# Differential attention: both score products of a step issued before both masks

## What is computed

```python
def _diff_attention(q, k, v, lam_params, subln_gain, layer_idx):
    q = q.reshape(bsz, seq, DIFF_HEADS, 2, DIFF_HEAD_DIM)   # 4 heads, 2 parts, 64
    k = k.reshape(bsz, seq, DIFF_HEADS, 2, DIFF_HEAD_DIM)
    ...
        mask = key_chunk[None, :] <= query_chunk[:, None]
        s1 = jnp.einsum('bhqd,bhkd->bhqk', q1_b, k1).astype(jnp.float32) * scale
        s2 = jnp.einsum('bhqd,bhkd->bhqk', q2_b, k2).astype(jnp.float32) * scale
        p1 = jax.nn.softmax(jnp.where(mask, s1, -jnp.inf), axis=-1)
        p2 = jax.nn.softmax(jnp.where(mask, s2, -jnp.inf), axis=-1)
        p = p1 - lam * p2
        return jnp.einsum('bhqk,bhkv->bhqv', p.astype(v.dtype), v)
```

## Time and profile before

| | us |
|---|---|
| median of three runs | 2064.28 |
| the profiled execution | 2043.03 |
| its span | 2041.2 |
| TensorE matmul busy | 1872.1 (92%) |
| VectorE busy | 1099.8 (54%) |
| ScalarE busy | 444.7 (22%) |
| GpSimd busy | 1059.1 (52%) |

### The profile page before, as it was taken

How to read it: one execution, slowest core, us unless ns; L and a number is a source line. 1 busy time by engine, 2 the same in 40 slices (tenths; PEclk the granted TensorE clock), 3 DMA queues, 4 the chain that set the end, 5 groups by cost and what they waited for, 6 DMA issues and landing times.

```text
span 2041.2 us, 22212 instructions
## 1 busy us (share of the span) xinstructions
PE 1872.1 (92%) x8206; PEld 1486.8 (73%) x8206; DVE 1099.8 (54%) x1235; ACT 444.7 (22%) x869; POOL 1059.1 (52%) x588
## 2 busy tenths in 40 slices
PE   7988897899999979997999999999856699999997
PEld 5865575678888867756888888887644588888885
DVE  7997528573442675165626344840566555344266
ACT  3213524420110131152201011101432222011011
POOL 7542253366666655504666666665500056666662
PEclk9989998899999989988999999999967699999999
DMA  5321121133333322301333333332200023333331
GB/s 202 92 72 42 42 73 52 42 93 93 103 93 94 101 83 77 94 1 52 94 102 93 95 101 93 94 101 86 83 0 0 0 82 94 93 101 95 93 103 42
DMA packets 45036, 160.55 MB, mean 79 GB/s; under 512 B 5136, under 2 KB 5648, under 8 KB 44832
## 3 DMA queue, kind: packets, MB, share of 16 engines
q1 hardware_dynamic: 43776, 157.31, 25.6%
q10 hardware_dynamic: 1184, 2.16, 0.3%
HBM read 157.35 MB, written 2.10 MB: 78 GB/s over the span
## 4 chain that ended last, share of the span: by engine, by line
PE 81%; DVE 13%; ACT 3%; issue 2%; DMA 0%; DVEq 0%; SPq 0%; ACTq 0%
PE bank L325 19%; PE bank L326 19%; PE bank L327 19%; PE bank L360 2%; PE bank L361 2%; PE bank L362 2%; DVE bank L1278 2%; DVE AL L1181 2%; PE bank L380 1%; PE bank L381 1%; PE bank L382 1%; PE bank L723 1%; PE bank L434 1%; PE bank L557 1%; PE bank L800 1%
## 5 line engine op out<-in xcount | busy, mean ns | idle before, releaser
L255 POOL TENSOR_SCALAR WH<-RAW 128x1024 fp32r<-128x1024 f32 x292 | 316.6, 1084 | 925.4 <-PE bank L327 410.0
L260 POOL TENSOR_TENSOR WL<-RAW,WH 128x1024 fp32r<-128x1024 f32 x292 | 742.6, 2543 | 24.4
L325 PE MATMUL bank<-AH,WH 128*128 128x512 f32 x944 | 369.6, 391 | 0.0
L326 PE MATMUL bank<-AL,WH 128*128 128x512 f32 x944 | 367.7, 390 | 0.0
L327 PE MATMUL bank<-AH,WL 128*128 128x512 f32 x944 | 367.7, 390 | 0.0
L325 PE MATMUL bank<-HH,WH 128*128 128x512 f32 x848 | 331.8, 391 | 0.0
L326 PE MATMUL bank<-HL,WH 128*128 128x512 f32 x848 | 330.4, 390 | 0.0
L327 PE MATMUL bank<-HH,WL 128*128 128x512 f32 x848 | 330.3, 389 | 0.0
L1482 DVE TENSOR_TENSOR HL<-TMP,HH 128x512 fp32r<-128x512 f32 x96 | 238.6, 2486 | 4.0 <-ACT HH L1052 0.8
L1047 ACT ACTIVATE TMP<-bank 128x512 f32<-128x512 f32 x96 | 57.2, 596 | 777.9 <-PE bank L327 739.2
L1488 DVE TENSOR_TENSOR Y<-Y,bank 128x512 f32<-128x512 f32 x72 | 49.5, 688 | 309.3 <-PE bank L327 309.3
(11 more groups left out here) (284 smaller groups left out, 2279.7 us busy)
## 6 DMA issues: line engine op xcount, KB each, us to landing
RAW<-wstream SPq DMA_DIRECT2D x292, 512.0 KB, 3.5
X<-xT SPq DMA_DIRECT2D x4, 512.0 KB, 7.4
out<-Y SPq DMA_DIRECT2D x8, 256.0 KB, 2.2
TMP<-memT ACTq DMA_DIRECT2D x1, 1024.0 KB, 9.1
BF<-masks ACTq DMA_DIRECT2D x1, 352.0 KB, 3.4
MIX<-pool_w ACTq DMA_DIRECT2D x1, 256.0 KB, 3.6
VC<-vecs ACTq DMA_DIRECT2D x1, 159.5 KB, 4.5
GM<-gla_masks ACTq DMA_DIRECT2D x1, 128.0 KB, 4.1
```

Source lines behind the costliest of these rows:

```text
L255: nc.gpsimd.tensor_scalar(WH[:, s, :, :].rearrange("p k n -> p (k n)"), RAW[:, s, :], 1.0, 1.0, ALU.mult, ALU.mult).then_inc(sem("w_high"), 1)
L260: nc.gpsimd.tensor_tensor(WL[:, s, :, :].rearrange("p k n -> p (k n)"), RAW[:, s, :], f32(WH[:, s, :, :].rearrange("p k n -> p (k n)")), A ...
L325: mm(bank, WH[:, slot, k, :], h(k), start=(k == 0), stop=False)
L326: mm(bank, WH[:, slot, k, :], l(k), start=False, stop=False)
```

## The change

TensorE's `attention` now issues all score products of a step first and collects their last instructions; if a `masked` function is given, it then issues the mask of each part, and the semaphore increments are put on these. The differential attention's score function is split in two for that, so that its order in a step is product 0, product 1, mask 0, mask 1 in place of product 0, mask 0, product 1, mask 1. The memory attention gives no `masked` and has one part a step, so its order is the same.

```diff
-            def attention(p, scores, values, o_place):
+            def attention(p, scores, values, o_place, masked=None):
...
+                        banks = [B[a["sbanks"][(i % rot) * subs + s]] for s in range(subs)]
+                        last = [scores(a["steps"][i], s, banks[s]) for s in range(subs)]
+                        if masked:
+                            last = [masked(a["steps"][i], banks[s]) for s in range(subs)]
                         for s in range(subs):
-                            bank = B[a["sbanks"][(i % rot) * subs + s]]
-                            scores(a["steps"][i], s, bank).then_inc(sem(f"{p}_scores"), 1)
+                            last[s].then_inc(sem(f"{p}_scores"), 1)
...
             def dif_scores(st, s, bank):
                 h, qt, kl = st
                 r = slice(s * 64, s * 64 + 64)
-                mm(bank[:, 0:kl], Q[r, h, qt * P:(qt + 1) * P], K[r, h, 0:kl], start=True, stop=False)
+                return mm(bank[:, 0:kl], Q[r, h, qt * P:(qt + 1) * P], K[r, h, 0:kl], start=True, stop=False)
+
+            def dif_mask(st, bank):
+                kl = st[2]
                 return mm(bank[:, kl - P:kl], BF[:, 0, :], BF[:, 2, :], start=False, stop=True)
             attention("dif", dif_scores, lambda h, kb: V[:, kb, h * P:(h + 1) * P],
-                      lambda h, qt, bank: bank[:, qt * P:(qt + 1) * P])
+                      lambda h, qt, bank: bank[:, qt * P:(qt + 1) * P], dif_mask)
```

## The result

The changed kernel took 2033.08 us (median of four, 2031.67 to 2041.14), the kernel before beside it 2063.92: a ratio of 0.9879, with a 95% interval of 0.9832 to 0.9926. It is faster by some 25 us (by the ratio) to 31 us (between the medians), where 4.6 were forecast and 2055.0 was the lowest time of the range. The two profiled executions lie only 9.6 us apart in span (2031.6 against 2041.2), so there are two questions: where these 9.6 come from, and where the other 20.

What follows compares the result with a forecast made beforehand. TensorE was taken to bound the differential attention; -2.6 us in the first stretch and -2.0 in two head loops gave -4.6, span 2036.6, and with 21.25 us carried over 2059.7 us, range 2055.0 to 2066.5.

Steps and rivals of the forecast that it cites:

- Step 2: Differential attention's two score products: second product's first record starts with the first's second; first mask after 1.6 us (512 keys).
- 3r: A step's two score products take three record times, not four; a step sheds 0.31 to 0.63 us.
- 2r: Outermost bound for a step's two score products: both run wholly together, in two record times.
- rival E: Both score products of a step wholly together: -9.6 us at most, 2054.7 us or later; chance 0.05.
- the 0.10 us: Score records on TensorE: a cost before every record that follows one on other or equal array rows.
- A: Score products: only the load is hidden, no overlap; sum -0.75 us, 2063.5 us; chance 0.18.
- B: The diff does nothing for the score products, still four record times; sum +0.5 us, 2064.8 us; chance 0.20.
- Step 3: VectorE's two maxima run back to back behind the masks, 0.61 us apart: +0.55 us a head, loop 10.1 us.
- Step 1: TensorE's masks: the second starts 0.07 us after the first, saving 0.10 us a step.
- Rival D: Products overlap and the attention's half-clock dip is shortened or gone: -5.6 to -9.6 us, 2054.7 to 2058.7; chance 0.13.
- Rival C: Products overlap, but TensorE idles over 1 us a head and later heads lose clock: +7.2 us, 2071.5; chance 0.07.
- The tail: After the differential attention's last scores, from 907.86 to the copy at 911.84: keeps its 3.98 us.

Runs made afterwards that it cites:

- version on the same rows: Changed kernel with both products of a step reading rows 0 to 63, so another output; median 2044.32 us, ratio 0.9933.
- late whole-row version: Kernel before with each product over all 128 rows (another output) and VectorE's first maximum also waiting for the second mask; median 2035.45 us.

## Why the prediction was wrong, point by point

1. **The base, the dearest mistake.** The sum was made against the profiled execution, and the 21.25 us by which the median lay above it were carried over as something at the ends that the edit does not touch. They were half clock inside the stage that the edit rewrites: 17.7 of them stand in the two profiles of the kernel before. The prediction had the price of a head at half clock, and all of its timed runs (2063.56 to 2065.37) lay 20 us above the profile, but it put the two together nowhere. Against its own profile the forecast was -4.6, measured -9.6 in span and -12.7 in the stage. Against the profile of a 2063.52 us execution the stage gives -30.4. At like clock the kernels are some 6 us apart, so the size of the forecast was near only for the smaller part of the gain.
2. **Step 2, how far the products overlap.** Taken at 3r, with 2r as the outermost bound and 0.05 of the chance (rival E). Measured 2r. The reasoning was that a product's second record stands in front of the other's first; in the trace the first records go together. By row, the savings per head are 0.74 (256 keys) and 0.94 us (384), from first record to where the transposes could start, and 1.21 us (512) to the mask that VectorE waits for; 2.89 in all, where 1.62 were taken (0.41 + 0.52 + 0.63 + 0.06). Of these 0.52 went back, most of it into new waits: 0.17 before the 512-key transposes at 890.31, which now wait for VectorE's combination, and 0.19 before their value products at 892.84, which now wait for ScalarE's copy. The head came out at 9.37 us, not 10.14. The Trainium skill, "TensorE: Matmul & The Clock Gate", section "Part 3: Packing small matmuls — row/col tiling", says that matmuls of other row groups start together, and the trace agrees (two records at 893.93). Its other half, that starts and ends keep program order, led the prediction to 3r, and that is not what was measured: the two products took 2r, so either the records are not issued product by product or the order does not hold for them; the trace can't tell which. The estimate from its table, 2.6r, was too careful for two products; by the terms of rival E it would have been worth 2.0 us, not 1.5.
3. **Step 2, the 0.10 us.** It was put on every record. It is 0.10 on entering a run and as much on leaving it, so two records of a product were a run of two, and a fit over two sizes couldn't tell "once a record" from "twice a run". For A and B this undersized the saving, as the version on the same rows showed (1.92 us for what B had at 2.1). The exception of the prediction, "the same cost with no change of mode", falls with it: inside a run no record paid the 0.10 us.
4. **Step 3, the late signal, was right.** One more maximum, 0.61 us, was forecast (+0.55 a head, with a first mask 0.06 earlier); by itself it cost 0.59 on whole rows (9.55 to 10.14) and 0.60 on the kernel before (11.15 to 11.75), and in the changed kernel the two maxima took 1.20 us where one took 0.61. It is 0.60 of the 1.05 us by which TensorE's idle time before the 384-key transposes rose (0.43 to 1.48 us). The rest is that the 128-key products, which fill part of that wait, now take 0.5 us less.
5. **Step 1** was right: the second mask follows the first by 0.06 us (894.99 to 895.05), and the transposes follow 0.12 us behind the first (895.11).
6. **The clock.** Rival D, the dip gone, had 0.13 and came true together with E (0.05); D was priced from the short dip, 5 us, E with the dip left as it was. Rival C, that idle TensorE lets the clock fall again for whole heads, is not borne out: the changed kernel idles 1.48 us a head and held 1.00 in one profile, the late whole-row version idles 1.56 and held it. A small part of it may be real: the three stretches of 3.4 us in the other profile of the changed kernel each began right behind a wait of 1.1 us or more, and made the stage 3.4 us longer. The prediction said that the clock went down in a stretch without idle time, but drew nothing from it for the length of the dip. What the runs show is that the long fall came in all four profiles with the old order on row halves in the first head, and in none of the eight others. In later heads the old order kept the full clock (41.6 us of it in the kernel with a changed first head), so half rows one after the other are not enough by themselves. Whether the rows bring the fall about, or the 0.10 us on entering and on leaving each run of them, is not separated: the same-rows version, half rows in fewer runs, held the clock in its first head and then lost it for 3.4 to 6.8 us at a time, 20.4 in all. Why one program can go either way after the fall stays open.
7. **The tail** kept its 3.98 us (897.84 to 901.82), as said.

## What to carry to other kernels

Before summing against a profiled execution, ask whether its time is that of the median; if not, the difference belongs to the sum, and the stretch where the clock is low with the engine busy is where it lay here. Here two products that use different row halves of the array and different banks cost one when they were next to each other (1.06 us) and two when a mask on the whole array stood between them. A change that gathers the work of one engine also gathers its signals: price what the next engine used to do meanwhile, here one maximum a head.

## What the runs showed of the hardware

- Two fp32 products of 64x128 by 64x512 on rows 0 to 63 and 64 to 127 took 1.06 us together, one alone 1.05 to 1.06; on the same rows 1.92.
- A run of half-row fp32 records took 0.21 us more than 0.427 us a record at full clock with 512 keys, for two records (1.06 us) and for four (1.92) alike; four whole-row records took 1.72.
- The granted clock fell from 1.00 to 0.50 some 4 us into a stretch of half-row fp32 products with TensorE busy nearly throughout (4.61 of 4.70 us, 3.80 of 3.80), and stayed down for 54.6 us in one execution of the same program and 13.7 in another, with TensorE busy all the time. A head costs 19.07 us at the one level and 11.15 at the other.
- TensorE idle for 1.5 us in every 9.4 to 10.1 us of the attention brought the clock down not at all (two profiles) or for 3.4 us at a time (the other profile of the changed kernel, each time 0.4 to 1.1 us behind a wait), where both halves or all of the rows were in use.
